# Order of half products and refills in the first expert pair, a split tenth load, a reordered routing chain and opening loads on two queues

## The chip, the cores and the metric

One core of one Trainium2 chip runs the whole kernel. The metric is device time in microseconds (us), lower is better; a time is the median of several executions. A measurement of this kernel cannot tell a difference of less than about 0.2% from none.

## The reference, cut to what matters

One step of a one-layer decoder: 272 prompt tokens (16 of them meta tokens) and 8 sampled tokens, 1024 channels, float32. A recurrent branch and an attention branch are merged through `w_out`; then every token is routed to 4 of 32 experts.

```python
z = rmsnorm(x) @ w_in                       # then the recurrent and the attention branch
x = x + merge(y_rnn, y_attn) @ w_out
logits = rmsnorm(x) @ w_router + b_router   # top 4 of 32, softmax over the 4
...
for e in range(32):                         # tokens of expert e
    z = xb @ w_up[e] + b_up[e]              # 1024 -> 2048
    y = x_glu * sigmoid(1.702 * x_glu) * (x_lin + 1)
    out += weight * (y @ w_down[e] + b_down[e])
```

The expert weights are 32 x 12 MB, and all of them are read.

## The kernel before, in words

**Trunk.** The sixteen 1 MB blocks of `w_in` and eight of `w_out` go through eight half slots of a ring (`block_full`), each refilled when the products with the block before have been issued. The first block comes in three parts, each beside a part of the tokens `x_cols` (lines 370 to 380): two quarters with two of the eight channel blocks each, then the rest. All these loads, and `vec` (the vectors of norms and biases) ahead of them, are issued on SP's queue; ACT's queue issues the load of `keep` (identity and slot numbers) at line 585. TensorE runs 14 products of ones (line 880, `keep_warm`) until the tokens come, then the products of line 1022 for the first block; `norm_sum` (line 887) waits for a chain of sums on DVE (lines 1393 to 1400), and after it TensorE waits for `keep`.

**Expert stage.** Experts are taken two at a time, 16 pairs. A pair has 12 loads of 2 MB: eight of `w_up` (numbers 0 to 7 of the first pair) and four of `w_down` (8 to 11); the second pair has 12 to 23. SP issues them all, in the order of its program, and each load waits by a semaphore until TensorE is done with what was in its place. There are ten places (eight ring slots and two areas, `EXTRA`) and a one-time place `front` for load 3. `wide_place(n)` gives the place of load n, `wide_before(n)` the load that was in it before, `WIDE_SLOT` the ring slot of a place. The loads 0, 1, 2, 4 to 10 fill the ten places; those for ring slots 0 to 3 wait for `wout_used`, which counts finished blocks of the output product (`out_block`, line 1086), so load 10 (slot 3) waits for the last one, and load 3 is issued behind it. Loads 11 to 15 come as two halves of 1 MB: the first half waits for `half_used`, the second for `ring_used`. From load 16 on each is one piece and waits for `ring_used`: load 16 takes the place of load 6, load 17 that of load 7. From the third pair on nine places are used (`nine_place`).

**First pair.** `pair(0, ..., first=True)` runs the `w_up` loads in `FIRST_ORDER`. Each load gives two halves of the contraction (`kk`), and each half is four products of 512 columns in float32, which the trace has as eight records of line 1284. Loads 0 to 3 (h = 0) make one half of the outputs, 4 to 7 (h = 1) the other. The inputs `xe` come in eight rows: `first_rows(j)` gathers row j with seven bf16 products (lines 1181 and 1184), into bank 6 or 7 in turn, and DVE scales it (line 1760, `xt_ready`). Rows 0 and 1 come ahead of the products, and two rows each behind the first three half products. The DVE function `gating(0)` clamps and gates the first outputs (lines 1719 to 1731); its buffers lie in `front`, so it waits until TensorE is done with load 3. `y_rows(0, 0)` (line 1218), behind load 6, transposes what it made.

**Routing.** Before the first pair: TensorE's logits (line 1119), copies to SBUF on DVE (lines 1650 and 1651), the logits as rows (`logit_rows`, line 1128), row norms, top 4 (lines 1661 to 1672), ranks within an expert (line 1157) and, behind them in the same bank and under one semaphore, the tokens of each expert (line 1161); then DVE's ranks and one-hot table (lines 1676, 1689), `slot_rows` (lines 1168, 1171) and the gathers.

The core of the refill order on SP, as it was:

```python
            if n <= WIDE + HALVED:
                turn = FIRST_ORDER.index(before)
                eng.wait_ge(s.half_used, turn - (turn > FIRST_ORDER.index(FRONT)) + 1)
                piece(n // PAIR_LOADS, n % PAIR_LOADS, dst, full, 0, SLOT // 2)
                eng.wait_ge(s.ring_used, turn + 1)
                piece(n // PAIR_LOADS, n % PAIR_LOADS, dst, full, SLOT // 2, SLOT)
```

Of the kernel before, what the change touches and what calls it, by code (L numbers as in the profile page):

```python
# [12 lines left out]

# [12 lines left out]
ALU = mybir.AluOpType  # L26
# [3 lines left out]
P = 128  # L30
# [106 lines left out]
def wide_place(n):  # L137

    return (n - (n > FRONT)) % WIDE


def wide_before(n):

    return n - WIDE - 1 if n - WIDE - 1 < FRONT else n - WIDE


def wide_parts(place, loads):

    return sum(2 if WIDE < n <= WIDE + HALVED else 1 for n in loads if n != FRONT and wide_place(n) == place)


def nine_place(n):

    return wide_place(WIDE_LOADS - WIDE + n % NINE)
# [16 lines left out]
extra_full0 extra_full1 front_full gamma_done gamma_ready router_loaded cache_loaded newkv_loaded zeroed consts_set squares sumsq rp_step half_full1 half_full2 half_full3 half_used rrow_done rrow_ready xe_ready  # L171
# [14 lines left out]
def program(nc, c_in, vec_cols, x_cols, conv_states, h_states, gate_w, key_cols, cache_k, cache_v, state_conv, w_in,  # L186
# [4 lines left out]
    with ctx:  # L191
# [122 lines left out]
        extra = (extra1[:, 0, :], extra0[:, 0, :])  # L314
# [54 lines left out]
        def _(eng):  # L369
            eng.dma_start(vec[:, :], vec_cols).then_inc(s.rows_loaded, 16)  # L370
            head = blocks[:, trunk_slot(0), :]
            for part, sem in enumerate((s.head_loaded0, s.head_loaded1)):
                c, k = slice(2 * COLS * part, 2 * COLS * (part + 1)), slice(2 * part, 2 * part + 2)
                eng.dma_start(head[:, c], w_in[0][:, c]).then_inc(sem, 16)
                eng.dma_start(x_raw[:, k, :], x_cols[:, k, :]).then_inc(sem, 16)
            eng.dma_start(x_raw[:, KB // 2:, :], x_cols[:, KB // 2:, :]).then_inc(s.xr_loaded, 16)
# [62 lines left out]
            for n in [n for n in range(WIDE + 1) if n != FRONT] + [FRONT]:  # L439
                if n == FRONT:  # L440
                    dst, full = front, s.front_full

                    eng.wait_ge(s.wout_used, KB)
                else:
# [4 lines left out]
                expert_dma(0, n, dst, full)  # L449

            for n in range(WIDE + 1, WIDE_LOADS):
                dst, full = place(wide_place(n))
                before = wide_before(n)
                if n <= WIDE + HALVED:
                    turn = FIRST_ORDER.index(before)
                    eng.wait_ge(s.half_used, turn - (turn > FIRST_ORDER.index(FRONT)) + 1)
                    piece(n // PAIR_LOADS, n % PAIR_LOADS, dst, full, 0, SLOT // 2)
                    eng.wait_ge(s.ring_used, turn + 1)
                    piece(n // PAIR_LOADS, n % PAIR_LOADS, dst, full, SLOT // 2, SLOT)
                else:  # L460
                    eng.wait_ge(s.ring_used, before + 1)
                    expert_dma(n // PAIR_LOADS, n % PAIR_LOADS, dst, full)
# [117 lines left out]
        def _(eng):  # L580
            act = eng.activation

            eng.wait_ge(s.consts_set, 2)
            act(stat[:, 15:16], eps[:, :], ACT.Exp)
            eng.dma_start(keep[:, :], c_in[:, 0:C_KEEP]).then_inc(s.consts_loaded, 16)
# [8 lines left out]
            act(sm[:, 8:16], sm[:, 0:8], ACT.Exp).then_inc(s.sp_exp, 1)  # L594
            eng.wait_ge(s.head_loaded1, 32)
# [278 lines left out]
        def _(eng):  # L874
# [8 lines left out]
            keep_warm(14, bank[7])  # L883
# [268 lines left out]
            for t in range(3):  # L1152
                m = P if t < 2 else TRIO
                for t2 in range(t + 1):
                    k = P if t2 < 2 else B_S
                    own = tri[0:k, 0:P] if t < 2 else tri[0:k, P:P + TRIO]
                    mm(bank[4][0:m, E_N * t:E_N * (t + 1)], own if t2 == t else ones[0:k, 0:m], selb[0:k, t2, :],
                       start=(t2 == 0), stop=(t2 == t))
# [98 lines left out]
            def first_rows(j):  # L1257

                if j >= 2:
                    eng.wait_ge(s.xt_ready, j - 1)  # L1260
                gather(0, (j,), 6 + j % 2).then_inc(s.gather_done, 1)

            def pair(q, full, pipelined, first=False, last=False, gamma=False):

                if first:

                    keep_warm(4, bank[7])
# [7 lines left out]
                for i in FIRST_ORDER if first else range(UP_LOADS):  # L1275
                    h = i // 4
                    w = full(i).rearrange("p (k e c) -> p k e c", k=2, e=2)
                    for kk in range(2):
                        k = 2 * (i % 4) + kk
                        if first and h == 0:  # L1280
                            eng.wait_ge(s.xt_ready, k + 1)
                        for n in range(2):
                            for e in range(2):
                                m = mm(bank[2 * h + n][64 * e:64 * e + 64, :], xe[:, k, 64 * e:64 * e + 64],  # L1284
                                       w[:, kk, e, NB * n:NB * (n + 1)], start=False, stop=(k == KB - 1),
                                       skip_group_check=True)
                                if kk == 1 and n == 1 and e == 1:
                                    m.then_inc(s.ring_used, 1)
                                elif k == KB - 1 and e == 1:
                                    m.then_inc(s.up_done, 1)  # L1290
                                elif first and i != FRONT and n == 1 and e == 1:
                                    m.then_inc(s.half_used, 1)
# [70 lines left out]
        def _(eng):  # L1363
# [303 lines left out]
            eng.tensor_scalar(ntop[:, 0:3], top[:, :, 0], -1.0, None, ALU.mult).then_inc(s.negtop, 1)  # L1667
# [4 lines left out]
            eng.tensor_tensor(selb[:, :, :], lg[:, :, 0:E_N], mr[:, :, 0:E_N], ALU.not_equal).then_inc(s.selb_ready, 1)  # L1672

# [79 lines left out]
            router_step(eng.tensor_reduce(cnt[0:1, 0, 0:1], bank[4][0:1, 3 * E_N:4 * E_N], AX.X, ALU.max))  # L1753
# [160 lines left out]
```

## Time and profile before

| what | value |
|---|---|
| median of 3 runs | 1147.6 us (1146.99 to 1148.8) |
| the profiled execution's own time | 1147.16 us |
| its span in the trace | 1145.4 us |
| TensorE busy | 97% of the span |
| moved by DMA | 437.90 MB, mean 382 GB/s |

The span is the trace from its first to its last instruction; 1.8 us of the execution's time lie outside it. The page also cuts the span into 40 slices of 28.6 us, with the share of time each engine and the DMA engines were busy. TensorE's busy time is modelled from pipelined products, so its 97% doesn't say that TensorE sets the time. An issue on a queue (SPq, ACTq) is the instruction that starts a transfer; "to landing" is from there until its semaphore.

### The profile page before, as it was taken

The page shows a single profiled execution, that of the slowest core. Times are in us where ns is not written, and L with a number is a line of the kernel's source. Part 1 is how long each engine was busy: PE and PEld are TensorE (multiplying, and loading weights), DVE is VectorE, ACT ScalarE, POOL GpSimd, SP SyncE. Part 2 cuts the span into 40 slices and gives each one's busy share as a digit, 9 for nine tenths or more (in the row PEclk, how much of TensorE's full clock was granted, in tenths as well). Part 3 has the DMA queues.
Part 4 walks back from the last instruction along what each step waited for, and adds up shares of the span by engine and source line. Part 5 has one row for each costly group of instructions (what it writes and reads, how often), then busy time and mean ns, then how long its engine had stood idle before and what let it go on. Part 6 is the DMA issues. An engine that isn't in the chain of part 4 may idle for free.

```text
span 1145.4 us, 14895 instructions
## 1 busy us (share of the span) xinstructions
PE 1113.8 (97%) x5772; PEld 493.7 (43%) x5772; DVE 311.7 (27%) x785; ACT 229.3 (20%) x642; POOL 33.8 (3%) x69
## 2 busy tenths in 40 slices
PE   9999999999999999999999999999999999999997
PEld 6687778844343424333333333333232323232432
DVE  6665543032131221212130303121212030312123
ACT  4564363422020202010101111111111101010103
POOL 0200012210000000000000000000000000000000
PEclk9999999999999999999999999999999999999999
DMA  9743636999999999999999999999999999999996
GB/s 349 281 142 107 187 112 270 391 375 427 428 427 427 426 427 427 427 429 427 429 428 429 429 428 429 429 428 428 429 429 429 428 428 429 429 428 425 427 426 244
DMA packets 39650, 437.90 MB, mean 382 GB/s; under 512 B 6592, under 2 KB 8912, under 8 KB 10944
## 3 DMA queue, kind: packets, MB, share of 16 engines
q1 hardware_dynamic: 38984, 435.65, 91.3%
q10 hardware_dynamic: 624, 1.68, 0.4%
q8 instruction: 28, 0.46, 0.2%
q14 instruction: 14, 0.11, 0.0%
HBM read 436.00 MB, written 2.41 MB: 383 GB/s over the span
## 4 chain that ended last, share of the span: by engine, by line
PE 69%; DMA 24%; DVE 3%; ACT 2%; issue 1%; DVEq 0%; SPq 0%; ACTq 0%
PE bank L1284 21%; DMA ring<-in_w_down 20%; PE bank L1328 19%; PE bank L1041 8%; PE bank L1086 5%; PE bank L1184 4%; DMA area<-in_w_down 3%; PE bank L1205 3%; PE bank L1134 2%; PE bank L1218 1%; PE bank L1181 1%; PE bank L1022 1%; PE bank L1208 1%; DVE area L1719 1%; PE bank L909 1%
## 5 line engine op out<-in xcount | busy, mean ns | idle before, releaser
L1284 PE MATMUL bank<-ring,area 128*64 128x512 f32 x1824 | 414.0, 597 | 9.8 <-DMA ring<-in_w_up 9.6
L1284 PEld LDWEIGHTS bank<-ring,area 128*64 128x64 f32 x1824 | 122.6, 136 | 273.3 <-issue 234.4
L1328 PE MATMUL bank<-ring,area 128*64 128x512 f32 x848 | 194.2, 598 | 6.4 <-DMA ring<-in_w_down 6.4
L1707 DVE TENSOR_TENSOR x_tok<-x_tok,bank 128x512 f32<-128x512 f32 x60 | 41.3, 688 | 328.0 <-PE bank L1205 328.0
L786 ACT ACTIVATE area<-area 128x256 f32<-128x256 f32 x64 | 26.7, 417 | 514.2 <-DVE area L1719 514.2
L1041 PE MATMUL bank<-ring 128*128 128x264 f32 (+1 forms) x512 | 121.7, 393 | 0.0
L1328 PEld LDWEIGHTS bank<-ring,area 128*64 128x64 f32 x848 | 57.8, 136 | 110.3 <-issue 92.4
L1041 PEld LDWEIGHTS bank<-ring 128*128 128x128 f32 x512 | 95.2, 190 | 21.3 <-issue 4.0
L1744 DVE TENSOR_TENSOR area<-area 128x1024 f32<-128x1024 f32 x15 | 18.4, 1225 | 211.3 <-ACT area L796 211.3
L1205 PE MATMUL bank<-area 128*128 128x512 f32 x128 | 71.8, 644 | 0.0
L1086 PE MATMUL bank<-area,ring 128*128 128x264 f32 x256 | 58.6, 387 | 0.0
L1184 PE MATMUL bank<-area,h_tok 128*128 128x128 bf16 x768 | 54.2, 219 | 0.0
L1086 PEld LDWEIGHTS bank<-area,ring 128*128 128x128 f32 x256 | 48.0, 190 | 8.8 <-issue 1.0
L1284 PE MATMUL bank<-area 128*64 128x512 f32 x224 | 50.9, 598 | 0.6 <-DMA area<-in_w_up 0.6
L796 ACT ACTIVATE area<-bank,vec 128x128 f32<-128x128 f32 x120 | 34.2, 368 | 82.5 <-PE bank L1184 82.5
L1184 PEld LDWEIGHTS bank<-area,h_tok 128*128 128x128 bf16 x768 | 48.9, 98 | 0.0
L1719 DVE TENSOR_SCALAR area<-bank 128x256 f32<-128x256 f32 x64 | 26.8, 419 | 79.4 <-PE bank L1284 79.3
L1328 PE MATMUL bank<-area 128*64 128x512 f32 x176 | 41.3, 601 | 1.6 <-DMA area<-in_w_down 1.6
L1205 PEld LDWEIGHTS bank<-area 128*128 128x128 f32 x128 | 19.1, 188 | 51.6 <-issue 51.6
L806 ACT ACTIVATE area<-bank 128x512 f32<-128x512 f32 x32 | 19.1, 597 | 82.7 <-PE bank L1218 82.7
L1284 PEld LDWEIGHTS bank<-area 128*64 128x64 f32 x224 | 15.0, 136 | 33.5 <-issue 28.6
L1181 PE MATMUL bank<-area,h_tail 72*128 72x128 bf16 x128 | 28.5, 223 | 0.0
(271 smaller groups left out, 712.6 us busy)
## 6 DMA issues: line engine op xcount, KB each, us to landing
ring<-in_w_up SPq DMA_DIRECT2D x112, 2048.0 KB, 33.2
ring<-in_w_down SPq DMA_DIRECT2D x49, 2048.0 KB, 31.6
area<-in_w_up SPq DMA_DIRECT2D x12, 2048.0 KB, 27.2
area<-in_w_down SPq DMA_DIRECT2D x11, 2048.0 KB, 31.8
ring<-in_w_in SPq DMA_DIRECT2D x16, 1024.0 KB, 9.4
ring<-in_w_out SPq DMA_DIRECT2D x8, 1024.0 KB, 4.9
ring<-in_w_down SPq DMA_DIRECT2D x7, 1024.0 KB, 37.1
area<-in_w_up SPq DMA_DIRECT2D x4, 1024.0 KB, 7.0
```

Of the source, the lines that this page charges most:

```text
L786: act(sig[:, n % 2, :], glu[:, n % 2, :], ACT.Sigmoid, scale=ALPHA).then_inc(s.sig_ready, 1)
L796: ins = act(xe[:, j, :], bank[half][:, P * i:P * (i + 1)], ACT.Copy, scale=vec[:, NFF + j:NFF + j + 1])
L1041: m = mm(proj_bank(n)[:, 0:T - lo], w[:, k, P * (n % 2):P * (n % 2) + P], (xn if n == 2 else h_t)[:, k, lo:T], start=(k == 0), stop=(k == ...
L1086: mo = mm(bank[m % 2][:, 0:NT], w[:, k, :], m_t[:, k, N_META:T], start=(k == 0), stop=(k == 2 * KB - 1))
L1134: mm(bank[b0 + n - n0][:, :], chosen[:, :], bias_parts[:, NB * n:NB * (n + 1)], start=True, stop=False, skip_group_check=True)
L1181: mm(out, h_tail[0:TRIO, P * j:P * (j + 1)], g_oh[0:TRIO, 2, :], start=True, stop=False)
L1184: m = mm(out, parts[:, t, i, P * j:P * (j + 1)], g_oh[:, t, :], start=False, stop=(t == 1 and i == 2))
L1205: m = mm(b[:, :], gw_t[:, lo:lo + P], yd[:, NB * c:NB * (c + 1)], start=True, stop=True)
L1284: m = mm(bank[2 * h + n][64 * e:64 * e + 64, :], xe[:, k, 64 * e:64 * e + 64], w[:, kk, e, NB * n:NB * (n + 1)], start=False, stop=(k == K ...
L1328: m = mm(bank[4 + c][64 * e:64 * e + 64, :], y_t[:, 4 * half + f, 64 * e:64 * e + 64], w[:, f, e, :], start=False, stop=(half == 1 and f = ...
L1707: eng.tensor_tensor(x, x, combined_bank(unit, last)[:, :], ALU.add).then_inc(s.added, 1)
L1719: eng.tensor_scalar(glu[:, n % 2, :], z[:, :, 0], LIMIT, None, ALU.min).then_inc(s.glu_ready, 1)
```

## The change

It reorders, splits and moves; no product, byte or output differs.

```diff
-EXTRA = (1, 2)
-WIDE_SLOT = {0: 4, 3: 5, 4: 6, 5: 7, 6: 0, 7: 1, 8: 2, 9: 3}
+EXTRA = (2, 3)
+WIDE_SLOT = {0: 4, 1: 5, 4: 6, 5: 7, 6: 0, 7: 1, 8: 2, 9: 3}
-FIRST_ORDER = (0, 1, 2, 4, 3, 5, 6, 7)
+FIRST_ORDER = (0, 4, 1, 2, 5, 3, 6, 7)
+FIRST_HALVES = ((0, 0), (4, 0), (0, 1), (4, 1), (1, 0), (1, 1), (2, 0), (2, 1), (5, 0), (5, 1), (3, 0), (3, 1),
+                (6, 0), (6, 1), (7, 0), (7, 1))
+RELEASED = (0, 4, 1, 2, 5, 6, 7, 8, 9, 10)
+AHEAD = ((4, 0), (4, 1), (1, 0), (1, 1), (2, 0), (2, 1))
...
+    return RELEASED.index(n) if n <= WIDE else (n - WIDE - 1) % WIDE          # wide_place
+    return RELEASED[n - WIDE - 1] if n - WIDE - 1 < WIDE else n - WIDE         # wide_before
...
# SP, opening: vec and the first quarter of w_in leave this queue, each x part goes ahead of its w_in part
-            eng.dma_start(vec[:, :], vec_cols).then_inc(s.rows_loaded, 16)
-                eng.dma_start(head[:, c], w_in[0][:, c]).then_inc(sem, 16)
                 eng.dma_start(x_raw[:, k, :], x_cols[:, k, :]).then_inc(sem, 16)
+                if part:
+                    eng.dma_start(head[:, c], w_in[0][:, c]).then_inc(sem, 16)
# ACT, opening
+            eng.dma_start(blocks[:, trunk_slot(0), 0:2 * COLS], w_in[0][:, 0:2 * COLS]).then_inc(s.head_loaded0, 16)
+            eng.dma_start(vec[:, :], vec_cols).then_inc(s.rows_loaded, 16)
             eng.wait_ge(s.consts_set, 2)
             act(stat[:, 15:16], eps[:, :], ACT.Exp)
-            eng.dma_start(keep[:, :], c_in[:, 0:C_KEEP]).then_inc(s.consts_loaded, 16)
...
             act(sm[:, 8:16], sm[:, 0:8], ACT.Exp).then_inc(s.sp_exp, 1)
+            eng.dma_start(keep[:, :], c_in[:, 0:C_KEEP]).then_inc(s.consts_loaded, 16)
# SP, expert loads: 0 to 9 without 3, then load 10 in halves, then load 3, then halves in order of release
+            dst, full = place(wide_place(WIDE))
+            for half in range(2):
+                eng.wait_ge(s.wout_used, KB - 1 + half)
+                piece(0, WIDE, dst, full, SLOT // 2 * half, SLOT // 2 * (half + 1))
+            expert_dma(0, FRONT, front, s.front_full)
+            for n, half in ((11, 0), (12, 0), (11, 1), (12, 1), (13, 0), (13, 1), (14, 0), (14, 1), (15, 0), (15, 1)):
+                half_load(n, half)          # half 0 waits for half_used, half 1 for ring_used, both turn + 1
# TensorE
-            keep_warm(14, bank[7])
+            keep_warm(12, bank[7])
# logit_rows: two waits in place of one
-                eng.wait_ge(s.router_step, 2)
+                eng.wait_ge(s.lt_ready, 1)
+                    if t == 2:
+                        eng.wait_ge(s.lt_ready, 2)
# the ranks get a semaphore step of their own; the counts go to bank 7 behind them
+            mr.then_inc(s.rank_done, 1)
-                m = mm(bank[4][0:1, 3 * E_N:4 * E_N], ones[0:k, 0:1], selb[0:k, t, :], start=(t == 0), stop=(t == 2))
+                m = mm(bank[7][0:1, 0:E_N], ones[0:k, 0:1], selb[0:k, t, :], start=(t == 0), stop=(t == 2))
             m.then_inc(s.rank_done, 1)
# first_rows
+                if j == 1:
+                    eng.wait_ge(s.flag_ready, 1)
-                    keep_warm(4, bank[7])
+                    keep_warm(4, bank[5])
# pair: the first pair's halves in FIRST_HALVES; one row behind each half of AHEAD
-                        if first and h == 0 and k < 3:
-                            first_rows(2 * k + 2)
-                            first_rows(2 * k + 3)
+                    if first and (i, kk) in AHEAD:
+                        first_rows(AHEAD.index((i, kk)) + 2)
# DVE
-            eng.tensor_copy(lt_trio, raw_lg[:, 2 * P:NT].unsqueeze(1).to_broadcast([P, 3, B_S]))
-            router_step(eng.tensor_copy(lt[:, 0:2 * P], raw_lg[:, 0:2 * P]))
-            eng.memset(lg[:, :, E_N:LG], MASKED)
+            eng.tensor_copy(lt[:, 0:2 * P], raw_lg[:, 0:2 * P]).then_inc(s.lt_ready, 1)
             eng.wait_ge(s.squares, 3 * KB)
             eng.tensor_reduce(stat[:, 0:3], ss[:, :, :], AX.X, ALU.add).then_inc(s.sumsq, 1)
+            eng.tensor_copy(lt_trio, raw_lg[:, 2 * P:NT].unsqueeze(1).to_broadcast([P, 3, B_S])).then_inc(s.lt_ready, 1)
+            eng.memset(lg[:, :, E_N:LG], MASKED)
-            eng.tensor_scalar(ntop[:, 0:3], top[:, :, 0], -1.0, None, ALU.mult).then_inc(s.negtop, 1)
...
             eng.tensor_tensor(selb[:, :, :], lg[:, :, 0:E_N], mr[:, :, 0:E_N], ALU.not_equal).then_inc(s.selb_ready, 1)
+            eng.tensor_scalar(ntop[:, 0:3], top[:, :, 0], -1.0, None, ALU.mult).then_inc(s.negtop, 1)
...
+            eng.wait_ge(s.rank_done, 2)
-            router_step(eng.tensor_reduce(cnt[0:1, 0, 0:1], bank[4][0:1, 3 * E_N:4 * E_N], AX.X, ALU.max))
+            router_step(eng.tensor_reduce(cnt[0:1, 0, 0:1], bank[7][0:1, 0:E_N], AX.X, ALU.max))
```

Left out: `wide_parts` counts load 10 as two parts, `nine_place` and `extra` are rewritten so that the same area is free at the end, and `half_load` and `views` are the loops above written out. `gating(0)` still waits for `FIRST_ORDER.index(FRONT) + 1` loads, which is now 6 in place of 5.

## Rows read from the trace of the kernel before

**Rows 1.** The page: GB/s in 40 slices of 28.6 us.

```profile
GB/s 349 281 142 107 187 112 270 391 375 427 428 427 427 426 427 427 427 429 427 429 428 429 429 428 429 429 428 428 429 429 429 428 428 429 429 428 425 427 426 244
```

**Rows 2.** The chain that ended last, in order of time: start us, us, what.

```profile
344.35 7.02 PE bank L1284 x32
...
399.32 7.02 PE bank L1284 x32
...
790.00 39.28 DMA ring<-in_w_down
...
848.74 39.30 DMA ring<-in_w_down
```

**Rows 3.** Windows: stretch, us, busy per engine, PEclk, DMA share, GB/s.

```profile
226.00:228.00 2.00, 2.00 (x10) 1.71 (x9) 0.00 (x0) 0.68 (x2) 0.72 (x2) 1.00 0.31 131
...
226.00:232.00 6.00, 5.24 (x28) 3.35 (x27) 1.82 (x11) 2.69 (x13) 0.97 (x4) 1.00 0.50 158
...
240.00:256.00 16.00, 16.00 (x95) 6.14 (x96) 3.69 (x13) 0.00 (x0) 0.00 (x0) 1.00 0.98 366
256.00:267.00 11.00, 11.00 (x55) 3.98 (x53) 3.03 (x8) 1.71 (x4) 0.00 (x0) 1.00 1.02 427
```

**Rows 4.** Timeline of SP's queue: issues of loads 10 and 16.

```profile
228.66 0.33 SPq L429 DMA_DIRECT2D ring<-in_w_down  x1
...
264.61 0.33 SPq L429 DMA_DIRECT2D ring<-in_w_up  x1
```

**Rows 5.** Issues of load 9 (line 429) and of the last half load (line 433), with landing.

```profile
L429 SPq DMA_DIRECT2D ring<-in_w_down x1: 328/328/328, 213.0 to 213.0; - x1
...
DMA to landing us min/median/max: 15.5/15.5/15.5
...
L433 SPq DMA_DIRECT2D ring<-in_w_up x1: 328/328/328, 261.2 to 261.2; - x1
...
DMA to landing us min/median/max: 7.7/7.7/7.7
```

**Rows 6.** Timeline of TensorE: first half product, a gather of two rows, the second half.

```profile
237.18 1.94 PE L1284 MATMUL bank<-ring,area 128*64 128x512 f32 x8 [0.21 <-DVE area L1760]
...
239.05 0.23 PE L1181 MATMUL bank<-area,h_tail 72*128 72x128 bf16 x1
...
239.45 0.22 PE L1181 MATMUL bank<-area,h_tail 72*128 72x128 bf16 x1
...
239.94 1.94 PE L1284 MATMUL bank<-ring,area 128*64 128x512 f32 x8
```

**Rows 7.** Timeline of DVE: first and last step of gating the first outputs.

```profile
257.75 0.42 DVE L1719 TENSOR_SCALAR area<-bank 128x256 f32<-128x256 f32 x1 [9.61 <-PE bank L1284]
...
260.13 0.75 DVE L1731 TENSOR_TENSOR area<-area 128x256 f32<-128x256 f32 x2
```

**Rows 8.** Timeline of the routing chain, 230 to 236 us.

```profile
230.36 0.18 DVE L1650 COPY area<-bank 128x24 f32<-128x24 f32 x1 [0.88 <-PE bank L1119]
...
230.46 0.41 DVE L1651 COPY area<-bank 128x256 f32<-128x256 f32 x1
...
232.81 0.17 DVE L1667 TENSOR_SCALAR area<-area 128x3 f32<-128x3 f32 x1
...
234.35 0.31 PE L1161 MATMUL bank<-area,ones 128*1 128x32 bf16 x3
...
235.61 0.23 PE L1168 MATMUL bank<-area,rt 72*128 72x128 bf16 x1
```

**Rows 9.** Windows of the opening, columns as in rows 3.

```profile
0.00:2.50 2.50, 1.50 (x4) 0.59 (x5) 0.14 (x3) 1.49 (x2) 1.96 (x14) 1.00 0.19 27
2.50:4.00 1.50, 1.50 (x5) 0.49 (x4) 0.51 (x3) 0.00 (x0) 0.02 (x1) 1.00 0.97 301
```

**Rows 10.** Timeline of the opening: first x load issued, first products.

```profile
1.68 0.43 SPq L375 DMA_DIRECT2D ring<-in_x_cols  x1
...
7.36 6.89 PE L1022 MATMUL bank<-ring 128*128 128x280 f32 x28 [1.42 <-ACT ring L588]
```

More of the change, by code:

```diff
@@ L14 @@
+import itertools
 from collections import namedtuple
@@ L137, in wide_place @@
 def wide_place(n):
-    return (n - (n > FRONT)) % WIDE
+    return RELEASED.index(n) if n <= WIDE else (n - WIDE - 1) % WIDE
 def wide_before(n):
-    return n - WIDE - 1 if n - WIDE - 1 < FRONT else n - WIDE
+    return RELEASED[n - WIDE - 1] if n - WIDE - 1 < WIDE else n - WIDE
 def wide_parts(place, loads):
-    return sum(2 if WIDE < n <= WIDE + HALVED else 1 for n in loads if n != FRONT and wide_place(n) == place)
+    return sum(2 if WIDE <= n <= WIDE + HALVED else 1 for n in loads if n != FRONT and wide_place(n) == place)
 def nine_place(n):
-    return wide_place(WIDE_LOADS - WIDE + n % NINE)
+    return wide_place(WIDE_LOADS + n % NINE)
 def nine_parts(n):
@@ L438, in _ @@
             eng.wait_ge(s.staged, 2)
[L439 to L444, printed above, removed]
+            for n in range(WIDE):
+                if n != FRONT:
                     dst, full = place(wide_place(n))
@@ L448, in _, with half_load @@
                         eng.wait_ge(s.wout_used, 2 * WIDE_SLOT[wide_place(n)] + 2)
-                expert_dma(0, n, dst, full)
-            for n in range(WIDE + 1, WIDE_LOADS):
+                    expert_dma(0, n, dst, full)
+            dst, full = place(wide_place(WIDE))
[3 more added lines that the diff above has]
+            expert_dma(0, FRONT, front, s.front_full)
+            def half_load(n, half):
+                before = wide_before(n)
+                turn = FIRST_ORDER.index(before)
+                dst, full = place(wide_place(n))
+                if half:
+                    eng.wait_ge(s.ring_used, turn + 1)
+                else:
+                    eng.wait_ge(s.half_used, turn + 1)
+                piece(n // PAIR_LOADS, n % PAIR_LOADS, dst, full, SLOT // 2 * half, SLOT // 2 * (half + 1))
+            for n, half in ((11, 0), (12, 0), (11, 1), (12, 1), (13, 0), (13, 1), (14, 0), (14, 1), (15, 0), (15, 1)):
+                half_load(n, half)
+            for n in range(WIDE + HALVED + 1, WIDE_LOADS):
                 dst, full = place(wide_place(n))
                 before = wide_before(n)
[L454 to L462, printed above, removed]
+                eng.wait_ge(s.ring_used, (FIRST_ORDER.index(before) if before < UP_LOADS else before) + 1)
+                expert_dma(n // PAIR_LOADS, n % PAIR_LOADS, dst, full)
             def behind(n):
@@ L1156, in _ @@
                     own = tri[0:k, 0:P] if t < 2 else tri[0:k, P:P + TRIO]
[L1157 to L1158 removed]
+                    mr = mm(bank[4][0:m, E_N * t:E_N * (t + 1)], own if t2 == t else ones[0:k, 0:m], selb[0:k, t2, :],
+                            start=(t2 == 0), stop=(t2 == t))
+            mr.then_inc(s.rank_done, 1)
             for t in range(3):
                 k = P if t < 2 else B_S
[L1161 removed]
+                m = mm(bank[7][0:1, 0:E_N], ones[0:k, 0:1], selb[0:k, t, :], start=(t == 0), stop=(t == 2))
             m.then_inc(s.rank_done, 1)
@@ L1274, in pair @@
                     biases(0, 4, 0)
[L1275 to L1292, printed above, removed]
-                        if first and h == 0 and k < 3:
-                            first_rows(2 * k + 2)
-                            first_rows(2 * k + 3)
@@ new lines, in pair @@
+                views = {}
+                for i, kk in FIRST_HALVES if first else itertools.product(range(UP_LOADS), range(2)):
+                    h, k = i // 4, 2 * (i % 4) + kk
+                    if kk == 0:
+                        views[i] = full(i).rearrange("p (k e c) -> p k e c", k=2, e=2)
+                    if first and h == 0:
+                        eng.wait_ge(s.xt_ready, k + 1)
+                    for n in range(2):
+                        for e in range(2):
+                            m = mm(bank[2 * h + n][64 * e:64 * e + 64, :], xe[:, k, 64 * e:64 * e + 64],
+                                   views[i][:, kk, e, NB * n:NB * (n + 1)], start=False, stop=(k == KB - 1),
+                                   skip_group_check=True)
+                            if kk == 1 and n == 1 and e == 1:
+                                m.then_inc(s.ring_used, 1)
+                            elif k == KB - 1 and e == 1:
+                                m.then_inc(s.up_done, 1)
+                            elif first and i != FRONT and n == 1 and e == 1:
+                                m.then_inc(s.half_used, 1)
+                    if first and (i, kk) in AHEAD:
+                        first_rows(AHEAD.index((i, kk)) + 2)
+                    if kk == 0:
+                        continue
```

4 lines of the change are left out of this document (2 added, 2 removed).

## The prediction

> **What bounds the kernel now.** I read the page's transfer rates first: from about 343 us on the core takes 425 to 429 GB/s to the end, below that there are holes, 375 GB/s in one slice [rows 1]. So the weights' transfers set the end, and it moves one for one with the time at which the stream stops having holes. The chain of waits agrees at its end: a pair takes 58.7 us between waits on transfers (790.00 to 848.74), while TensorE's own pace in the earlier pairs is 55.0 us (344.35 to 399.32) [rows 2]. TensorE is slower than the stream in nothing but the start: there it has not freed places yet, and SP may not issue.
>
> The windows give the holes. Against 428 GB/s, 226 to 232 us lacks 6 x (428 - 158) / 428 = 3.8 us, 240 to 256 us lacks 16 x (428 - 366) / 428 = 2.3 us, and 256 to 267 us nothing [rows 3]. The first: loads 0 to 9 are in, and load 10 is issued only at 228.66, behind the last output block [rows 4]. The second: from the first product on, half loads are freed every 2.76 us (239.94 - 237.18 [rows 6]) while one takes 2.45 us (1.05 MB at 428 GB/s). Together 6.1 us; the question is how much of that can be had.
>
> **The limit behind the holes.** Load 16 is still one piece and waits until TensorE has done seven loads: 264.61 [rows 4]. From a lone issue to data: load 10 is issued at 228.66; the data before it end near 226.6 (2 us at 131 GB/s are 0.6 us at the full rate), the hole is 3.8, so its data flow as from 230.4, 1.75 us behind the issue [rows 3, 4]. Load 16 could so begin at 266.35. The stream reached it at 267.0: the last half before it landed at 261.2 + 7.7 = 268.9 [rows 5], and a landing comes some 1.9 us behind the last data, as load 9's did (213.0 + 15.5 = 228.5 against 226.6) [rows 3, 5]. So load 16 has 0.65 us of slack, no more. A hole filled ahead of it is opened again in front of it, unless TensorE gets there earlier. Bounds for the slack: 0 (if the delay is 2.4) to 1.2 (if it is 1.2). The Trainium skill, DMA: Bandwidth & Descriptors (Anatomy of one DMA), gives a fixed cost of about 2.0 us for a DMA, most of it at completion. Taken whole as the delay it would leave 0.4 us of slack in place of 0.65.
>
> **Tenth load in halves.** Its first half waits for seven output blocks, and so is issued a whole output block earlier, beside running data; it fills 2.45 of the 3.8 us. The second half and load 3 behind it on SP keep their times, and load 3 is ready long before its turn. **Halves in order of release.** With the two loads 0 and 4 side by side, half products free 1 MB each at about 1.7, 3.5, 5.9 and 7.6 us from the first product, in place of 2.0, 4.7, 7.5 and 10.3, so the later halves no longer lag. The stream is 2.45 us ahead by then, and load 11 can't be issued more than some 1.2 us earlier, so a part of the first hole comes back in front of it, about 2.6 us. Of the second hole I leave 0.7 for small losses. Holes left by my sum: 1.35 + 2.6 + 0.7 = 4.65 of 6.1. The stream alone would then be at load 16 about 1.5 us earlier, before what the start gains. But this is not what is collected, since load 16's release comes later than that.
>
> **What TensorE gains and loses up to load 16.** Three terms, and they decide.
>
> *Opening.* Before, the first x part is issued third, at 1.68 [rows 10]; now first, at about 0.74, with its quarter of `w_in` beside it on ACT's queue. The DMA engines are busy 19% of the first 2.5 us and 97% of the next 1.5 us [rows 9]: what can be won is in the first stretch and in the 224 KB of `keep`, which now come later (about 0.5 us at full rate, partly given back, as they then run beside the rest of the first block). The first products, at 7.36 [rows 10], may come over 1 us earlier, but they run into the rest of the block and into the sums on DVE, which need the later x parts. I take 0.45 us. Bounds: 1.4 (0.94 of earlier issue and `keep`'s 0.5, all passed on) and -0.2 (x beside a rival, and `vec` now last: DVE's three small steps come after it). The Trainium skill, DMA: Bandwidth & Descriptors (Issuing engines are not separate DMA queues), says that queues share the same 16 engines, and that a second issuer saves only the time to initiate. By that the 0.94 us is all that this part can save, and less once the engines are full; the 97% agrees. [...] The two DMA issues and the later table load on ACT lie in its wait for x. `keep` is needed behind `norm_sum`, well after it lands. Two products of ones less keep TensorE free for the earlier start; if x is late they cost nothing.
>
> *Routing.* The long copy goes first, 0.10 us (230.36 against 230.46); the norms' sum and the short copy follow beside TensorE's first two row products. `ntop` leaves the chain: its record is 0.17, of which 0.12 counts. The ranks' semaphore no longer waits for the counts: 0.31 us of records, about 0.23 of them behind the ranks; but TensorE's order (counts, four products of ones, then `slot_rows` at 235.61) is unchanged, so of this 0.14 is left [rows 8]. Sum 0.36. Bounds 0 and 0.5. `ntop` later delays ACT's exponentials by 0.3 us; they lie under a wait for POOL's split. The new wait of row 1 for the flag has TensorE's queue behind it, but the flag is made during `slot_rows` and row 0; without that cover it would be 0.2 us.
>
> *Gathers.* A half product takes 1.72 us (32 such records take 7.02, the overhang of the last one among them [rows 2], so 8 take a little under 1.75). A break for two rows then lasts 239.94 - 237.18 - 1.72 = 1.04 us, of which a row takes 0.40 (239.45 - 239.05), so a break itself costs 0.24 [rows 6]. Three breaks for six rows become six: 6 x 0.64 - 3 x 1.04 = +0.72 us. Bounds: 0 (the fixed part hides) and 3.1 (a break for one row costs as much as for two). No row has a break of one row.
>
> TensorE reaches load 16's release 0.45 + 0.36 - 0.72 = 0.09 us earlier. `gating(0)` starts one load later; it took from 257.75 to 260.88 [rows 7], 3.1 us, and load 6's 3.44 us of products cover it just before `y_rows`. If not, a few tenths fall on load 17, whose slack is larger (1.0).
>
> **Sum.** 0.09 + 0.65 = 0.74 us. The profiled execution took 1147.16, its span 1145.4; so 1146.4 for one like it. It lies 0.44 under the median, which gives 1147.6 - 0.7 = 1146.9.
>
> **Rivals.**
> 1. *Stream decides, not load 16.* If the slack is the full 1.2 and the opening passes on 1.2, load 16 comes 1.2 + 0.84 = 2.0 us earlier: 1145.6. For it: what the holes add up to; against it: 264.61 so close to 267.0. With every bound at its best, 1.2 + 1.4 + 0.5 = 3.1: 1144.5. Chance 0.2 for gains over 1.4.
> 2. *The queues are no gain.* The opening gives 0: 0.3 us in all, 1147.3. Chance 0.22. [...]
> 3. *Breaks cost more (slower).* Where a break for one row costs b, TensorE loses 6b - 3.12. Place: between the halves before load 16's release. From b = 0.76 on the kernel is slower than before (6b - 3.12 over 0.65 + 0.81). At b = 1.04 it is 3.12 - 1.46 = 1.7 us slower: 1149.3. For it: TensorE's weight loads idle at each change; against it: the two rows inside a break follow at 0.40. Chance 0.08.
> 4. *It doesn't do what it says:* the first half of load 10 is issued no earlier. Then only its 2.45 us are missing in the stream, load 16 starts about as before, time within 0.3 of 1147.6. Chance 0.02.
>
> My forecast, gains of 0.3 to 1.4, has the rest, 0.48.
>
> **How the numbers follow.** 0.2% is 2.3 us, about what a measurement of this kernel can tell from no change. Faster by more needs nearly every bound at once: 0.14. Slower by more needs rival 3 and an opening that loses: 0.03. The rest, 0.83, is within it. The range goes from 1145.0 (rival 1) to 1148.1 (rivals 2 and 3 in part, and the 0.5 us by which the median itself moves).
>
> **What would show it.** Right: load 10's first half issued a block ahead of 228.2, near 220.5; the hole at 226 to 232 down to about 1.4 us; a new hole of 2 to 3 us ahead of load 11; load 16 issued within 0.5 us of 264.6, with a hole or nearly one before its data; first products near 6, single breaks of 0.6. Wrong: load 16 issued over 1 us earlier, or breaks near 1.0, or the stream full from 232 on.

## The result and the profile after

The changed kernel takes 1159.57 us (median of 4, 1158.79 to 1159.71) against 1147.76 us (median of 4, 1146.99 to 1148.8) for the kernel before, run beside it: a ratio of 1.0097, interval 1.0085 to 1.011. It is slower by 11.8 us, well outside the forecast range. The profiled execution took 1159.66 us, its span is 1157.8 us.

Lines of the page of the kernel after, with its rates and queues (its GB/s row is to be read against [rows 1]). q8 is one of the two queues that the page marks `instruction`; the page of the kernel before has 28 packets and 0.46 MB there.

```profile
PE 1116.4 (96%) x5770; PEld 495.0 (43%) x5770; DVE 311.7 (27%) x785; ACT 230.0 (20%) x642; POOL 34.0 (3%) x69
...
PE   8999999999999999979999979999979999999997
...
GB/s 352 250 157 110 185 111 274 417 361 399 428 428 426 428 427 426 428 427 426 427 427 427 428 427 427 426 427 429 426 428 427 426 428 427 427 427 427 428 422 144
...
q8 instruction: 55, 0.90, 0.3%
```

Three things are to be seen. The rates are full from the eleventh slice on (before: 427 GB/s in the tenth already, here 399), so whatever costs most of the 11.8 us is no hole of the stream in the long middle of the run. TensorE's row has a 7 in three slices, evenly spaced, where it had a 9. And q8 moved 27 more packets, 0.44 MB, 16 KB each.

The waits of TensorE, after (engine, line, releaser: us in total, times, longest):

```profile
PE bank L1151 <- issue: 24.7, 6, 5.3
PE bank L1236 <- DVE area L1752: 4.5, 15, 0.4
PE bank L1037 <- ACT ring L602: 2.5, 1, 2.5
```

The waits of TensorE, before:

```profile
PE bank L1284 <- DMA ring<-in_w_up: 9.6, 36, 0.4
PE bank L1328 <- DMA ring<-in_w_down: 6.4, 10, 0.8
PE bank L1218 <- DVE area L1731: 2.3, 8, 0.4
PE bank L1328 <- DMA area<-in_w_down: 1.6, 2, 0.8
PE bank L1022 <- ACT ring L588: 1.4, 1, 1.4
...
PE bank L1284 <- DMA area<-in_w_up: 0.6, 3, 0.2
```

"Issue" means that nothing which the profile shows released the instruction. The line is that of `biases`, the first products of a pair. The timeline of TensorE shows where; after (start us, us, what, idle before it):

```profile
506.91 3.65 PE L1349 MATMUL bank<-ring,area 128*64 128x512 f32 x16
513.45 0.39 PE L1151 MATMUL bank<-bias_parts,chosen 96*128 96x512 bf16 x1 [2.89 <-issue]
519.13 1.46 PE L1151 MATMUL bank<-bias_parts,chosen 96*128 96x512 bf16 x3 [5.30 <-issue]
520.52 4.64 PE L1304 MATMUL bank<-area 128*64 128x512 f32 x16
...
688.59 0.39 PE L1151 MATMUL bank<-bias_parts,chosen 96*128 96x512 bf16 x1 [3.07 <-issue]
694.13 1.46 PE L1151 MATMUL bank<-bias_parts,chosen 96*128 96x512 bf16 x3 [5.16 <-issue]
...
864.80 0.60 PE L1151 MATMUL bank<-bias_parts,chosen 96*128 96x512 bf16 x1 [3.07 <-issue]
870.61 1.46 PE L1151 MATMUL bank<-bias_parts,chosen 96*128 96x512 bf16 x3 [5.21 <-issue]
```

and before, at the same place of the program:

```profile
504.63 3.65 PE L1328 MATMUL bank<-area 128*64 128x512 f32 x16
508.22 1.04 PE L1134 MATMUL bank<-bias_parts,chosen 96*128 96x512 bf16 x4
509.19 7.09 PE L1284 MATMUL bank<-ring,area 128*64 128x512 f32 x32
```

TensorE's program runs twelve of the pairs in a loop of four turns with three pairs in its body. The three stops are at the starts of the sixth, ninth and twelfth pair, that is at each jump back to the head of the loop: some 8.2 us each, in two pieces with one product between them. Nine packets of instructions belong to each (27 / 3), but not all nine to the stop itself. q8 in the window 500 to 530 us of the kernel after:

```profile
q8 instruction: 3, 0.05, 0.6%
```

Three packets lie around the first stop, and 6 more come one by one over the rest of that turn, 530 to 680 us. The kernel before makes the same jumps without a stop, and its q8 moves nothing at all from 505 to 1000 us.

The stops also cost some pace. Windows after the second stop (columns as in [rows 3]):

```profile
695.60:700.00 4.40, 4.40 (x12) 1.32 (x14) 0.00 (x0) 0.00 (x0) 0.00 (x0) 0.50 1.01 425
700.00:704.00 4.00, 4.00 (x22) 1.35 (x20) 0.00 (x0) 0.00 (x0) 0.00 (x0) 0.99 0.99 422
```

The granted clock is 0.50, the lower of the two levels (1.2 GHz against 2.4), for some 4 us after TensorE had stood idle; the first 32 products of these pairs take 8.01, 9.24 and 8.05 us in place of 7.02 in the chain.

**The account.** Idle time of TensorE, span less busy time: 1145.4 - 1113.8 = 31.6 us before (its busy time is on its page), 1157.8 - 1116.4 = 41.4 after, so +9.8. The waits give just that: +24.7 for the stops, +2.2 at the transposes (line 1236, more often waiting since TensorE is now the later one), +1.1 in the opening, and -18.2, all the waits for transfers, which are gone (9.6 + 6.4 + 1.6 + 0.6). Busy time grew by 2.6 us. The slow restarts are in it (the first 32 products behind the three stops alone take 4.2 us more), and other rows got shorter; that split was not taken further. The kernel before with nothing but the 12 products, below, grows by 2.8 us. 9.8 + 2.6 = 12.4, the difference of the spans. So the stops are not paid in full: TensorE runs a pair in 55.0 us and the stream in 58.7 [rows 2], and the first stops eat that reserve. After them TensorE is the late one to the end: transfers have 24% of the chain that ended last in the kernel before and 0% in the one after. And the last two slices of the rates (422 144 against 426 244) show that the data end earlier than the work by more than before.

### The profile page after: what moved, and what is told of

Same layout as the page of the kernel before. It is cut to its first block, busy times and chain, and to the rows that moved or that the text cites. A ratio compares the mean times of both kernels' runs of the same rounds, so it can differ in the third digit from the quotient of the medians.

```text
span 1157.8 us, 14892 instructions
## 1 busy us (share of the span) xinstructions
PE 1116.4 (96%) x5770; PEld 495.0 (43%) x5770; DVE 311.7 (27%) x785; ACT 230.0 (20%) x642; POOL 34.0 (3%) x69
## 4 chain that ended last, share of the span: by engine, by line
PE 89%; DVE 4%; issue 4%; ACT 2%; DMA 0%; DVEq 0%; ACTq 0%
PE bank L1304 35%; PE bank L1349 20%; PE bank L1056 8%; PE bank L1223 6%; PE bank L1101 5%; PE bank L1202 4%; PE bank L1151 2%; PE bank L1236 2%; PE bank L1226 1%; DVE area L1740 1%; PE bank L1199 1%; DVE area L1752 1%; PE bank L1037 1%; ACT area L801 1%; PE bank L924 1%
## 5 line engine op out<-in xcount | busy, mean ns | idle before, releaser
L1304 PE MATMUL bank<-area 128*64 128x512 f32 x304 | 73.8, 627 | 0.0
L1151 PE MATMUL bank<-bias_parts,chosen 96*128 96x512 bf16 x96 | 28.9, 408 | 24.7 <-issue 24.7
L1304 PEld LDWEIGHTS bank<-area 128*64 128x64 f32 x304 | 21.7, 145 | 46.1 <-issue 45.7
L1151 PEld LDWEIGHTS bank<-bias_parts,chosen 96*128 96x128 bf16 x96 | 7.1, 100 | 55.3 <-issue 51.1
```

What stands on the lines that cost most here:

```text
L1151: mm(bank[b0 + n - n0][:, :], chosen[:, :], bias_parts[:, NB * n:NB * (n + 1)], start=True, stop=False, skip_group_check=True)
```

## The experiments

**Which part brings the stops.** The description of the change says that no product differs, and that is not quite so: it removes two products of ones in the opening, the only products of TensorE that go (x5772 to x5770 on the page). Each has its weight load, so everything behind them, the loop too, lies four instructions earlier in the code. The change also adds two waits of TensorE ahead of the loop; the runs on the kernel before, below, have none of them.

The change with 14 products:

```diff
-            keep_warm(12, bank[7])
+            keep_warm(14, bank[7])
```

> The changed kernel with 14 products of ones in the opening again, so TensorE has as many instructions ahead of its loop over pairs as before. Theory (place of the code): the stops of 8.2 us of TensorE at the start of every third pair go, the fetches of instructions (queue q8) fall from 55 to about 28, and the time is 1148.7 us, within 0.7: what is left is the late opening (1.7 us at the first pair) and the dearer breaks. Rival (the stops come from the order of the loads, as a refill lands late): they stay, time 1159 to 1160.

Measured 1149.27 us (10 runs) against 1147.86 (25 runs), ratio 1.001 (1.0001 to 1.002). The page and TensorE's waits:

```profile
q8 instruction: 28, 0.46, 0.2%
...
PE bank L1304 <- DMA ring<-in_w_up: 8.9, 36, 0.4
PE bank L1349 <- DMA ring<-in_w_down: 7.6, 11, 0.8
```

The stops are gone, the waits for transfers are back. 10.3 of the 11.8 us are undone by two products that compute nothing.

The kernel before with 12 products:

```diff
-            keep_warm(14, bank[7])
+            keep_warm(12, bank[7])
```

> The kernel before with 12 products of ones in place of 14 and nothing else. Theory (place of the code): three stops of about 8 us at the start of pairs 5, 8 and 11, some 27 more fetches on q8, time 1157 to 1158.5 us. Rival (the stops belong to the new order): no stop, 1147.7 us within 0.5.

Measured 1157.74 us (4 runs, 1157.24 to 1158.81), ratio 1.0088 (1.0071 to 1.0105):

```profile
q8 instruction: 55, 0.90, 0.3%
...
PE bank L1134 <- issue: 23.6, 6, 5.6
```

So this edit alone, without anything else of the change, brings the stops, the 27 packets and 9.9 us.

**Is it the place of the code or the opening?** The change with 12 products in the opening and two more of the same in the routing stage, ahead of the loop all the same:

```diff
-            keep_warm(6, bank[0])
+            keep_warm(8, bank[0])
```

> The changed kernel with 12 products of ones in the opening, and two more of them later, behind the logits as rows (8 in place of 6). The opening is the changed one, only the place of the loop's code is that of before. Theory (place of the code): no stops, 1149.1 us within 0.8, as in the run with 14 and up to 0.4 more for the two products. Rival (the clock or the start in the opening makes the stops): they stay, 1159 to 1160.

Measured 1149.43 us (10 runs), ratio 1.0015 (1.0005 to 1.0025); 28 packets, no stop, first products at 7.41. So it is the number of instructions that counts, not when they run or what the clock does in the opening. No run puts the two products behind the loop, so that it is their place ahead of the loop, and not the length of TensorE's whole program, is argued and not shown.

One product less (kernel before, 13 in place of 14):

> The kernel before with 13 products of ones, a shift of its loop by one load and one product. Theory (the body's start must lie in a window): before lies at most four instructions behind the lower edge, so either no stop and about 1147.8 us (edge two or more away) or three stops and about 1157.7 us; nothing in between. Rival (the stops grow with what is taken away): about half the loss, 1152.8.

Measured 1158.12 us (one run) against 1147.85, 55 packets, three stops, here each in one piece of up to 8.8 us, 25.9 us of "issue" in all. Two instructions are enough, and the loss does not grow with their number. More instead of fewer, 8 and then 16 small products of ones (32 columns) behind the 14 (in the diff 8, in the second run 16):

```diff
             keep_warm(14, bank[7])
+            for _ in range(8):
+                mm(bank[7][:, 0:E_N], ones[:, :], ones[:, 0:1].to_broadcast([P, E_N]), start=True, stop=True)
```

> The kernel before with eight small products of ones (32 columns) more behind the 14: 16 instructions more ahead of the loop. Theory: a body of three pairs has about 1767 instructions of TensorE (852 loads and 852 products as records, 63 others as built), 25 short of seven blocks of 256, and before starts within the first four of such a window: still inside, no stop, 28 fetches, 1147.3 to 1148.8 us. Rival (any other place than that of before is bad): stops, 1157.7.

> The kernel before with sixteen small products of ones more: 32 instructions more ahead of the loop, past the upper edge of the window of 25. Theory: three stops of about 8 us, some 55 fetches, 1157 to 1158.5 us, though here work was added ahead of the loop and not taken away. Rival (only a shift towards the front stops it): no stop, 1148.

With 8 (16 instructions) the one run gives 1149.62 us, 28 packets and no stop. The time is 0.8 us above the expected range; its first products came late, at 7.70, and one run does not say more. With 16 (32 instructions) the one run gives 1150.41 us and a result that neither theory had, 37 packets and a single stop, at the jump in the middle:

```profile
677.18 1.89 PE L1136 MATMUL bank<-bias_parts,chosen 96*128 96x512 bf16 x4 [4.02 <-issue]
```

Nine packets more again, but half the stop. So there seems to be a second edge somewhere beyond 16 instructions, and by this one trace it is less sharp than the lower one. Why one jump of three stops there stays open.

**The opening.** `vec`, now second on ACT's queue, is late. Timeline after:

```profile
1.20 0.46 ACTq L597 DMA_DIRECT2D vec<-in_vectors  x1
...
6.95 0.17 DVE L1404 TENSOR_SCALAR area<-vec 128x8 f32<-128x8 f32 x1 [5.99 <-DMA vec<-in_vectors]
6.95 0.53 ACT L602 ACTIVATE ring<-ring,vec 128x280 f32<-128x280 f32 x1 [3.76 <-DMA vec<-in_vectors]
...
7.62 7.58 PE L1037 MATMUL bank<-ring 128*128 128x280 f32 x25 [2.52 <-ACT ring L602]
```

It is used at 6.95, 5.7 us after its issue. Before, it was issued at 0.74 and used 2.3 us later, and x set the start:

```profile
3.02 0.17 DVE L1383 TENSOR_SCALAR area<-vec 128x8 f32<-128x8 f32 x1 [2.06 <-DMA vec<-in_vectors]
```

The first part of x did come earlier: it landed at 4.65 (issued at 0.75, 3.9 us to landing), before at 6.58 (1.68 and 4.9). The change with 14 products and `vec` ahead of the quarter of `w_in` on ACT's queue:

```diff
+            eng.dma_start(vec[:, :], vec_cols).then_inc(s.rows_loaded, 16)
             eng.dma_start(blocks[:, trunk_slot(0), 0:2 * COLS], w_in[0][:, 0:2 * COLS]).then_inc(s.head_loaded0, 16)
-            eng.dma_start(vec[:, :], vec_cols).then_inc(s.rows_loaded, 16)
```

> The changed kernel with 14 products of ones, and on ACT's queue vec ahead of the first quarter of w_in. Theory (vec behind 256 KB on its queue, beside SP's loads, is what made the opening late): vec lands near 3 us in place of 6.9, the first products start near 6 us, TensorE's clock stays at 2.4 GHz, the first expert product is 1.5 to 2.5 us earlier than in the run with 14 alone, and the time 1 to 2 us lower, 1146.5 to 1147.7. Rival (the engines' rate sets the opening): first products still near 7.4, time within 0.5 of the run with 14 alone.

Measured 1149.10 us (10 runs), ratio 1.0011 (1.0002 to 1.0021), against 1149.27 with `vec` second:

```profile
3.98 0.17 DVE L1404 TENSOR_SCALAR area<-vec 128x8 f32<-128x8 f32 x1 [3.02 <-DMA vec<-in_vectors]
...
7.05 0.53 ACT L602 ACTIVATE ring<-ring,vec 128x280 f32<-128x280 f32 x1 [3.87 <-DMA ring<-in_w_in]
...
7.73 6.61 PE L1037 MATMUL bank<-ring 128*128 128x280 f32 x27 [0.72 <-ACT ring L602]
```

`vec` comes 3 us earlier and nothing is won: now the quarter of `w_in` lands last, at about the same time. My theory that `vec` held the start fell. The first products need all three, x, `vec` and the quarter of `w_in`, and the last of the three lands at 6.6 us before, 6.9 in the changed kernel and 7.0 with `vec` first. What the two queues have in common is the rate behind them. The windows of the opening after, against [rows 9]:

```profile
0.00:2.50 2.50, 1.50 (x4) 0.58 (x5) 0.14 (x3) 0.81 (x1) 1.96 (x14) 1.00 0.24 24
2.50:4.00 1.50, 1.50 (x5) 0.55 (x4) 0.00 (x0) 0.68 (x2) 0.04 (x1) 1.00 0.90 270
```

The earlier issues bring no more data in these 4 us (24 GB/s against 27 in the first 2.5 us, 270 against 301 in the next 1.5); they only change which piece lands first. That a small load issued beside large ones gets only its share of the rate is my reading of this; no row shows the shares.

The change with the opening as before and 14 products (routing, order and tenth load stay):

> The changed kernel with the whole opening of before (vec, w_in and x loads all on SP in the old order, keep at ACT's start, 14 products of ones). Left of the change: routing chain, tenth load in halves, half products and refills in order of release. Theory (TensorE's release of load 16 decides; the new opening costs 0.2 us): first expert product at 237.0 (0.2 ahead of before), load 16 issued near 265.2, holes of the stream by 290 us 7.1 in place of 6.1 us, time 0.2 lower than the run with 14 ones alone, 1148.7 to 1149.3. Rival (the stream decides): 1 to 1.5 us lower than before.

Measured 1149.02 us (11 runs) against 1147.85 (33 runs), ratio 1.0008 (0.9999 to 1.0017). Each taken against its own runs of before, the new opening costs 1.41 - 1.17 = 0.24 us, which is not clear of noise (each of the two ratios is known to about 0.1%, 1 us). That it gains nothing is clearer from the starts: the first products come at 7.41 to 7.73 us in the five traces with the new opening, and at 6.73 to 7.36 in eight of the nine with the old one (the ninth is the 7.70 above).

**Rows by two.** The same with the rows gathered two at a time again, three breaks in place of six:

```diff
-AHEAD = ((4, 0), (4, 1), (1, 0), (1, 1), (2, 0), (2, 1))
+AHEAD = ((4, 0), (4, 1), (1, 1))
...
-                        first_rows(AHEAD.index((i, kk)) + 2)
+                        first_rows(2 * AHEAD.index((i, kk)) + 2)
+                        first_rows(2 * AHEAD.index((i, kk)) + 3)
```

> As e5_opening_back, with the rows of the input gathered two at a time again (behind the halves (4,0), (4,1) and (1,1)), so three breaks in place of six. Theory: load 16 is issued 0.7 us earlier than in e5_opening_back and the time falls by 0.7, to 1148.0 to 1148.5, about that of before. Rival (a break costs nothing that counts): the same time as e5_opening_back.

Measured 1147.65 us (11 runs), ratio 0.9998 (0.9989 to 1.0007): 1.37 us better than the run above, twice what the breaks themselves cost and more than was expected. (The two profiled executions are 0.92 us apart.) A single break, in the timeline after:

```profile
246.87 1.94 PE L1304 MATMUL bank<-area 128*64 128x512 f32 x8
248.74 0.23 PE L1199 MATMUL bank<-area,h_tail 72*128 72x128 bf16 x1
248.81 0.50 PE L1202 MATMUL bank<-area,h_tok 128*128 128x128 bf16 x6
249.24 1.94 PE L1304 MATMUL bank<-area 128*64 128x512 f32 x8
```

249.24 - 246.87 - 1.72 = 0.65 us, as forecast. A good part of the rest shows at loads 16 and 17. The windows with single rows (the run before this one) and with rows by two:

```profile
267.00:272.00 5.00, 5.00 (x24) 1.46 (x22) 3.27 (x9) 0.83 (x2) 0.00 (x0) 1.00 0.98 387
272.00:278.00 6.00, 6.00 (x34) 2.07 (x31) 0.14 (x1) 0.60 (x1) 0.00 (x0) 1.00 0.93 380
```

```profile
267.00:272.00 5.00, 5.00 (x25) 1.32 (x20) 3.41 (x9) 0.83 (x2) 0.00 (x0) 1.00 0.98 411
272.00:278.00 6.00, 6.00 (x37) 2.39 (x36) 0.00 (x0) 0.62 (x2) 0.00 (x0) 1.00 0.99 401
```

These 11 us lack 1.15 us of data at 428 GB/s with single rows (5 x 41/428 + 6 x 48/428) and 0.58 with pairs of rows: my reading is that TensorE frees each place later, and more than one load pays.

**The tenth load alone.** The kernel before with nothing but load 10 in two halves:

```diff
+                elif n == WIDE:
+                    dst, full = place(wide_place(n))
+                    for half in range(2):
+                        eng.wait_ge(s.wout_used, KB - 1 + half)
+                        piece(0, WIDE, dst, full, SLOT // 2 * half, SLOT // 2 * (half + 1))
```

> The kernel before with the tenth load in halves and nothing else: its first half is issued one output block earlier. Theory (a hole filled ahead opens again in front of load 16): the hole at 226 to 232 us falls from 3.8 to 1.4 us, new ones come by 270 us, the sum of holes stays at 5.2 to 6.1, gain 0 to 0.9 us (1147.0 to 1147.9). Rival (the stream decides): gain of the whole 2.45 us, 1145.4.

Measured 1148.04 us (11 runs), ratio 1.0001 (0.9992 to 1.001). Its windows, against [rows 3]:

```profile
226.00:232.00 6.00, 5.24 (x28) 3.25 (x27) 2.13 (x12) 2.99 (x14) 0.93 (x5) 1.00 0.87 329
...
236.00:242.00 6.00, 5.79 (x51) 2.84 (x49) 1.57 (x5) 1.97 (x3) 0.46 (x2) 1.00 0.58 199
242.00:256.00 14.00, 14.00 (x83) 5.27 (x81) 3.33 (x11) 0.00 (x0) 0.00 (x0) 1.00 1.00 373
256.00:267.00 11.00, 11.00 (x57) 4.01 (x55) 3.03 (x8) 1.71 (x4) 0.00 (x0) 1.00 1.03 429
```

The hole at 226 to 232 shrinks from 3.8 to 1.4 us. A new one of 3.2 us opens at 236 to 242, ahead of load 11, and 1.8 us follow. The sum is 6.4 us; it was 6.1. The stream waits for TensorE in front of load 11 for what it had won in front of load 10. That the stream decides (rival 1), which would have left the 2.45 us in the time, fell.

**Halves for loads 16 and 17.** The rows by two, the opening as before, and two more loads in halves:

```diff
-HALVED = 5
+HALVED = 7
...
-                    eng.wait_ge(s.half_used, turn + 1)
+                    eng.wait_ge(s.half_used, turn - (turn > FIRST_ORDER.index(FRONT)) + 1)
...
-            for n, half in ((11, 0), (12, 0), (11, 1), (12, 1), (13, 0), (13, 1), (14, 0), (14, 1), (15, 0), (15, 1)):
+            for n, half in ((11, 0), (12, 0), (11, 1), (12, 1), (13, 0), (13, 1), (14, 0), (14, 1), (15, 0), (15, 1),
+                            (16, 0), (16, 1), (17, 0), (17, 1)):
```

> As e6_rows_by_two, with loads 16 and 17 in halves too, so that their first halves need not wait for a whole load of TensorE's. Theory (load 16 decides): its first half is issued 1.7 us earlier, the holes ahead of loads 16 and 17 go, the holes' sum falls to 5 us or less and the time by 1 us or more against e6_rows_by_two, to 1146.5 to 1147.3, below both kernels. Rival (loads 18 and later decide, or half loads cost rate): within 0.4 us of e6_rows_by_two.

Measured 1147.23 us (11 runs, 1146.53 to 1147.88), ratio 0.9993 (0.9984 to 1.0002), 0.4 us below the rows by two. In its windows 267 to 278 us run at 425 GB/s. The theory wanted 1 us or more and fell; the rival's 0.4 is about what came, and between these two medians 0.4 us is not clear of noise. It is the fastest version found, 0.6 us below the kernel before, but its interval includes no difference.

**The change again, unaltered**, for the clock of the opening:

> The changed kernel once more, unaltered, for a second trace. Whether TensorE's clock in its opening falls each time: theory (12 products end too early for the late vec, the gap before the first product is over 2 us each time): clock at 0.5 to 0.9 again from 7 to 12 us and the first expert product near 238.7. Rival (chance of where the activity falls): full clock, first expert product near 237.2, and the time 0 to 1 us lower. The three stops are there in both.

Measured 1158.59 us (one run), 55 packets, 25.1 us of "issue". Windows of 7 to 10 us, the profiled execution after, then this run:

```profile
7.00:10.00 3.00, 2.38 (x5) 1.85 (x6) 1.94 (x6) 2.74 (x6) 0.00 (x0) 0.52 1.01 410
```

```profile
7.00:10.00 3.00, 2.56 (x11) 2.14 (x12) 1.91 (x5) 2.74 (x6) 0.00 (x0) 1.00 1.04 423
```

In the first, the 12 products of ones were done after 4.10 us and TensorE stood idle for 2.52 us; the clock then was 0.52, near the lower level. Here they took 5.30 us, the gap was 1.13 us and the clock stayed at 1.00. The first expert products start at 237.02 in place of 238.70 (237.18 before). The products of `norm_sum`, behind the first block, start at 15.75 in the first and at 14.11 here, so the delay of 1.6 us arises in just this stretch. So the 1.5 us by which the first profile was late at the first pair came with this fall of the clock. It doesn't come in every execution (the run with the two products shifted has the same opening, a gap of 1.14 us and a clock of 1.00); the stops are in both traces of the changed kernel.

## Why the prediction was wrong, by its own steps

**The step that failed** is one sentence on the opening: "Two products of ones less keep TensorE free for the earlier start; if x is late they cost nothing." It weighed their time and not their place in the code. Shown: this edit alone adds 9.9 us to the kernel before, putting them back takes 10.3 us from the changed one, and two such products elsewhere ahead of the loop do the same. The stops come with 9 packets of 16 KB on the instruction queue for each turn that a stop begins. That they are fetches of the loop's own code is read from these packets and from the stops' places; no row names the code fetched. The trace of the kernel before shows three jumps back, and three turns behind them, without a packet on q8 and can't say how near that is to an edge, but an edit that shifts a loop's code deserved bounds of its own, and a rival.

The Trainium skill, Runtime: NRT & Kernel Launch (Instruction fetch mechanics), says that instructions are fetched sequentially in 16 KiB blocks, and that a taken branch to a target outside the current window of two pages forces a fetch of that page before execution goes on. The packets' size and the stops agree. The window does not: a turn brings 9 packets where it is fetched, far more than two pages, so by it every one of these jumps would stop; here the same loop shows three stops, one, or none, by its place.

**Opening, +0.45.** Not collected: it measured -0.24 us, near the lower bound of -0.2, and not told from nothing. The first products came at 7.4 to 7.7 in place of 6. The 0.94 us of earlier issue brought x earlier by 1.9 us, and `vec` or the quarter of `w_in` later, as the lower bound had it. As far as these runs tell, rival 2, no gain, holds for this part. Besides, with 12 products one of three traces had a 2.52 us gap and the fall of the clock behind it, which there cost some 1.5 us.

**Routing, +0.36.** The same profile gives 0.2: the last output block ends 1.7 us late, the first expert product 1.52 (238.70 - 237.18). Half of it came, and this one is firm: from the issue of load 3, which waits for the last output block, to the first expert product it takes 8.14 or 8.15 us in four traces with the old chain and 7.96 to 7.98 in seven with the new one.

**Gathers, -0.72.** The size on TensorE was right: from the first expert product to the issue of load 16 it took 28.20 us (266.90 - 238.70) against 27.43 (264.61 - 237.18 [rows 4, 6]), 0.77 more, and single breaks of 0.65. But in time they cost 1.37; that load 17 is late with load 16 would explain it, and the windows above show about half of the difference there.

**Holes and slack.** The mechanism was right, and the run with the tenth load alone shows it: 1.4 us left of the first hole, and the rest back ahead of load 11. Its signs came too: load 10's first half was issued at 220.46 in the second trace of the changed kernel. But load 16 was issued at 265.22 there, a little over 0.5 us late, since the opening gave nothing and the routing chain half.

The slack of load 16, +0.65, was collected in small part. With rows by two, load 16 is issued at 264.65, before at 264.61. By 267 us the stream lacks 5.3 us of data there, against 6.1 before, and then gives 0.6 back at loads 16 and 17, where the kernel before loses 0.1. That leaves 0.3, about what the time shows (0.2). The delay on which the 0.65 rested is not firm either. It took 1.75 us from issue to data and 1.9 from data to landing, which with 4.9 us of data makes 8.6 us for a load that waits for nothing. The traces have from 8.0 us (issued at 265.51, with `vec` first) over 9.2 (before) to 10.9. So the slack itself may be larger than 0.65; what keeps it from being collected is the small losses (410 GB/s in place of 428 in 267 to 272 us), and their cause stays open. Halves for loads 16 and 17 remove them (425 GB/s), for another 0.4 us that is not clear of noise.

**Sum without the code's place.** The change with 14 products was to gain 0.74 us and lost 1.4. The difference of 2.15 us by the medians of these runs: opening 0.7 (+0.45 to -0.24), gathers 0.65 (0.72 to 1.37), and 0.8 missing for routing, order and slack together, of 1.01 expected (the rows by two stand 0.2 below the kernel before). Of the three only the gathers' 1.37 is clear of noise as a time.

## What to carry to other kernels

Before and after any edit on an engine whose program has a long loop, compare the packets of the instruction queue and look for stops with the releaser "issue" at the loop's first line; if they appear, add or remove a few harmless instructions ahead of the loop and measure again. Price a removed instruction by where it puts the rest of the code as well as by its time. And where one engine's releases bound a stream, a hole filled ahead of a release opens again in front of the next: shorten the work up to the release, or free smaller pieces.

## What the hardware showed that was not expected

- Two instructions less ahead of TensorE's loop turn three free jumps into three stops of 7.7 to 8.8 us with 9 packets of 16 KB for each turn; 16 more bring no stop; 32 more give one stop of 4.02 us (one run each). In windows over the stops of the changed kernel the DMA engines move 423 to 432 GB/s.
- After such a stop the granted clock is 0.50 for up to 4.4 us. In the opening, a gap of 2.52 us was followed by 0.52, gaps of 1.13, 1.37 and 1.56 us by 1.00.
- A small load issued 0.45 us behind 256 KB on the same queue, with another queue busy, was usable 5.7 us after its issue; ahead of it, 3.2 us; ahead of everything on one queue, 2.3 us.
